# A hybrid encoder trunk on one core: the softmax shift folded into the low product of the scores, new orders in the attention, and the last down-projection turned round

## The reference

```
h = rms_norm(x); p = h @ W_in                       # 1024 -> 1952 columns
A: Hyena on 256 channels (FFT convolutions, gates)
B: GQA, 8 query heads, 2 key/value heads of 64      softmax(q k^T / 8) v
C: MLA, 4 heads, query/key 64 + 32 rotary, value 64 softmax(q k^T * 96^-0.5) v
x += rms_norm(concat(norm A, norm B, norm C) @ W_out)
h = rms_norm(x)
x += rms_norm((gelu(conv(h W_g)) * conv(h W_u)) @ W_down)   # 2816 wide inside
```

## Time and profile before

| | |
|---|---|
| median of 3 runs | 1431.39 us (1431.07 to 1433.14) |
| the profiled execution's own time | 1426.5 us |
| its span in the trace | 1424.7 us |
| PE busy | 1368.3 us, 96% of the span |
| DVE, ACT, POOL busy | 64%, 41%, 39% |

### The profile page before, as it was taken

The page is one execution under the profiler, slowest core; times in us unless marked ns, Lnnn a source line. Parts: engine busy times, 40 slices in busy tenths (PEclk is TensorE's granted clock), DMA queues, the critical chain, the costliest instruction groups (busy, mean ns, idle before and its releaser), DMA issues. The chain is left out here.

```text
span 1424.7 us, 15494 instructions
## 1 busy us (share of the span) xinstructions
PE 1368.3 (96%) x5988; PEld 1027.0 (72%) x5988; DVE 915.4 (64%) x992; ACT 587.7 (41%) x864; POOL 554.1 (39%) x287
## 2 busy tenths in 40 slices
PE   7999989999999999999989998998999999999998
PEld 5587654378888888788866785444888888887886
DVE  6776976547777787611286788665478877874213
ACT  5322455545543434422352225454464344343323
POOL 3221333046444444444552224320554444444444
PEclk9999999999999999999999999999999999999999
DMA  7313201022233333233341222110223333333332
GB/s 250 97 30 81 67 10 52 1 61 73 85 94 95 97 89 103 82 93 95 101 143 49 60 49 57 30 30 15 75 75 89 89 99 94 89 99 87 92 97 84
DMA packets 205538, 112.53 MB, mean 79 GB/s; under 512 B 15303, under 2 KB 202425, under 8 KB 204570
## 3 DMA queue, kind: packets, MB, share of 16 engines
q1 hardware_dynamic: 205466, 111.54, 27.0%
HBM read 105.63 MB, written 2.10 MB: 76 GB/s over the span
## 5 line engine op out<-in xcount | busy, mean ns | idle before, releaser
L527 POOL TENSOR_TENSOR wl<-raw,wh 128x1024 fp32r<-128x1024 f32 x172 | 421.5, 2451 | 628.2 <-ACT wh L611 628.2
L611 ACT ACTIVATE wh<-raw 128x1024 fp32r<-128x1024 f32 x172 | 182.1, 1059 | 519.8 <-PE ps L1140 493.8
L1138 PE MATMUL ps<-gh,wh 128*128 128x512 f32 (+1 forms) x848 | 340.7, 402 | 0.0
L1140 PE MATMUL ps<-gh,wl 128*128 128x512 f32 (+1 forms) x848 | 334.7, 395 | 0.0
L1139 PE MATMUL ps<-gl,wh 128*128 128x512 f32 (+1 forms) x848 | 334.6, 395 | 0.0
L1138 PEld LDWEIGHTS ps<-gh,wh 128*128 128x128 f32 (+1 forms) x848 | 158.3, 187 | 43.3 <-issue 3.9
L1139 PEld LDWEIGHTS ps<-gl,wh 128*128 128x128 f32 (+1 forms) x848 | 158.3, 187 | 40.5 <-issue 2.4
L1140 PEld LDWEIGHTS ps<-gh,wl 128*128 128x128 f32 (+1 forms) x848 | 158.2, 187 | 39.1
L1599 DVE TENSOR_TENSOR acc<-acc,sq 128x512 f32<-128x512 f32 x24 | 60.2, 2510 | 190.1 <-ACT sq L655 190.1
L2030 DVE SCALAR_TENSOR_TENSOR cv<-pad,pm,cv 128x512 f32<-128x512 f32 x88 | 127.4, 1447 | 70.0 <-ACT cv L989 70.0
L1138 PE MATMUL ps<-fh,wh 128*128 128x512 f32 x308 | 121.7, 395 | 0.6 <-POOL wl L527 0.6
(11 more groups left out here) (288 smaller groups left out, 2242.0 us busy)
## 6 DMA issues: line engine op xcount, KB each, us to landing
raw<-w_up SPq DMA_DIRECT2D x86, 512.0 KB, 3.8
raw<-w_down SPq DMA_DIRECT2D x32, 512.0 KB, 3.8
raw<-w_in SPq DMA_DIRECT2D x30, 512.0 KB, 4.1
raw<-w_out SPq DMA_DIRECT2D x16, 512.0 KB, 3.8
raw<-w_down SPq DMA_DIRECT2D x16, 384.0 KB, 3.4
xio<-x SPq DMA_DIRECT2D x4, 512.0 KB, 4.7
win<-c_win SPq DMA_DIRECT2D x2, 1024.0 KB, 5.5
TF<-c_tf SPq DMA_DIRECT2D x2, 1024.0 KB, 8.7
```

The costliest lines, as they stand in the source:

```text
L527: nc.gpsimd.tensor_tensor(l, raw[:, slot, :], h.bitcast(F32), ALU.subtract).then_inc(S["lo_ready"], 1)
L611: A(xh[:] if third(lay, n) else wh[:, slot, :], raw[:, slot, :], ACT.Copy).then_inc(S["hi_ready"], 1)
L1138: mm(ps[0:cols, bank, :], w_hi, x_hi, start=start and k == 0, stop=False)
L1140: ins = mm(ps[0:cols, bank, :], w_lo, x_hi, start=False, stop=stop and k == tile_n - 1)
```

## The change

**Scores.** `diag`, `shift` and the matmul of ones by `diag` are gone. The high half of a GQA head's keys still meets the packed query. The low half of the keys now meets a new tile `q3`: rows 0 to 63 hold the query (copied by POOL, `q_again`), rows 64 to 67 hold four rows, one for each block of 128 queries, with the negated maxima in that block and zero elsewhere; the keys' rows 64 to 67 are ones. So one matmul of 68 rows does the low product and the shift. An MLA head does the same in rows 96 to 99 of its one float32 matmul. To get the maxima as rows, PE multiplies the 128x4 tile `nm` by the identity (`turn_maxima`, 128 columns, float32, after `scores(h - 1, 3)`), and DVE spreads them (`max_row`).

**Orders.** `values(p, [2])` stays at the end of the even head; `values(p, [3])` moves to the odd head ahead of `denominators(p)`. In the last head `values(5, [0])` comes ahead of `denominators(4)`. Two of the four `mla_lo` subtractions move from DVE to POOL; the other two, `rotate_kr`, some `row_sums`, the squares and norms of the output groups and the splitting of the first two W_out items change places. `klo` writes each half once instead of twice, and ones into four rows.

**Layer 1's down-projection.** Its items are now 22 blocks of 128 rows of W_down. The activations are stationary and the weights move, so all 8 PSUM banks hold the result with tokens on partitions. The last two items are multiplied bank by bank, so that the banks end one after the other. ACT squares a bank with an accumulated sum, takes the logarithm and the exponential of one column, DVE applies gain and root and adds the old stream, and each of 8 pieces goes out. The old stream is transposed beforehand, four transposes at a time in eight of layer 1's feed-forward steps (`turn_stream`), and copied by ACT into buffers that are free.

The diff, cut to its core:

```
@@ pool
-                def shift(h):
-                    pool.wait_ge(S["nmax"], lay * N_TILES + (h + 1) * TC)
+                def q_again(h):
+                    pool.wait_ge(S["q2hi"], lay * GH + h + 1)
                     if h >= 2:
                         pool.wait_ge(S["s_tile"], lay * N_TILES + (h - 1) * TC)
-                    nc.gpsimd.tensor_tensor(diag[:, h % 2, :].rearrange("p (c n) -> p c n", c=TC), ..., ALU.mult)
+                    nc.gpsimd.tensor_copy(q3[0:GD, h % 2, :], qf[(h % 2) * GD:(h % 2 + 1) * GD, h // 2, :])
...
+                q_again(0)
+                q_again(1)
+                for k, (dst, src, hi_) in enumerate(((uql, uqr, uqh), (ukl, ukr, ukh))):
+                    nc.gpsimd.tensor_tensor(dst[:], src[:], hi_[:].bitcast(F32), ALU.subtract).then_inc(S["mlo_w"], 1)
                 q_lo(2)
@@ tensor
+                def turn_maxima(h):
+                    pe.wait_ge(S["nmax"], lay * N_TILES + (h + 1) * TC)
+                    mm(ps[ROW(h), N_BANK(h, TC - 1), 0:P], nm[:, h % 2, :], ident[:], start=True, stop=True)
...
                     if h < GH:
                         mm(ps[:, bank, :], ka[:, h // 4, keys], Q2[h % 3], start=True, stop=False)
-                        mm(ps[:, bank, :], kb[:, h // 4, keys], Q2[h % 3], start=False, stop=False)
+                    if sc == 0:
...
+                        pe.wait_ge(S["nm_row"], lay * HEADS + h + 1)
+                    if h < GH:
+                        ins = mm(ps[:, bank, :], kb[row, h // 4, keys], q3[row, h % 2, :], start=False, stop=True)
                     else:
-                        mm(ps[:, bank, :], mkf[0:MD, h - GH, keys], mqf[0:MD, h - GH, :], start=True, stop=False)
-                    if sc == 0:
-                        pe.wait_ge(S["shift"], lay * HEADS + h + 1)
-                    mm(ps[:, bank, :], ones_r[:], diag[:, h % 2, :], start=False, stop=True).then_inc(S["s_tile"], 1)
+                        ins = mm(ps[:, bank, :], mkf[row, h - GH, keys], mqf[row, h - GH, :], start=True, stop=True)
...
                     scores(h, 3)
+                    if after:
+                        turn_maxima(h + 1)
                     if whole:
-                        values(p, [2, 3])
+                        values(p, [2])
+                    if rest:
+                        values(p, [TC - 1])
+                    if h == HEADS - 1:
+                        values(PAIRS - 1, [0])
                     if rest:
                         denominators(p)
...
+                    if lay == DEPTH - 1 and 4 <= j < 20 and j % 2 == 0:
+                        turn_stream((j - 4) // 2)
...
+                for kk in range(FC - TAIL):
+                    ready(kk)
+                    for tt in (0, 2, 3, 1):
+                        for dh in range(2):
+                            ins = part(kk, tt, dh)
+                    ins.then_inc(S["pe_item"], 1)
+                for kk in range(FC - TAIL, FC):
+                    ready(kk)
+                for tt in range(TC):
+                    for dh in range(2):
+                        for kk in range(FC - TAIL, FC):
+                            ins = part(kk, tt, dh)
+                        ins.then_inc(S["y_done"], 1)
@@ vector
+                def max_row(h):
+                    dve.wait_ge(S["nm_tr"], lay * HEADS + h + 1)
+                    tt(dst.rearrange("p (c n) -> p c n", c=TC),
+                       ps[rows, N_BANK(h, TC - 1), 0:P].unsqueeze(1).to_broadcast([TC, TC, P]),
+                       ident[rows, rows].unsqueeze(2).to_broadcast([TC, TC, P]), ALU.mult).then_inc(S["nm_row"], 1)
@@ vector, after the layers
+            for i in range(TC):
+                for dh in range(2):
+                    dve.wait_ge(S["y_sq"], 2 * i + dh + 1)
+                    tt(ytmp[dh], ps[:, 2 * i + dh, :], cv[:, dh, :], ALU.mult).then_inc(S["y_gain"], 1)
+                dve.wait_ge(S["r_inv"], i + 1)
+                for dh in range(2):
+                    stt(out=x, in0=ytmp[dh], scalar=st[:, i, 4:5], in1=x, op0=ALU.mult, op1=ALU.add).then_inc(S["o_done"], 1)
```

More of the change, by code:

```diff
@@ L255, in build @@
             krs = sb("krs", [P, T], F32, s)
[L256 removed]
+            q3 = sb("q3", [P, 2, T], F32R, s)
             q2c = sb("q2c", [P, T], F32R, s)
@@ L264, in build @@
         ysave = probT0
+        xres = [rope[:, i, :] for i in range(5)] + [w3[:, 0:T], w3[:, T:2 * T], h2[:, 0:T]]
+        ytmp = [sq[:, 0, :], sq[:, 1, :]]
         groot = [rbc[:], cv[:, 1, :], rbc[:]]
@@ L502, in _ @@
             res = out.rearrange("b (c p) d -> p (b c) d", p=P)
[L503 to L507, removed]
+            for tt in range(TC):
+                for dh in range(2):
+                    sp.wait_ge(S["o_done"], 2 * tt + dh + 1)
+                    sp.dma_start(res[:, tt, dh * T:(dh + 1) * T], xres[2 * tt + dh]).then_inc(S["out_sem"], 16)
             sp.wait_ge(S["out_sem"], 16 * DC)
@@ L1009, in _ @@
                 tables("natural_log_exp_and_others")
+                if lay == DEPTH - 1:
+                    for n in range(I_DOWN + 3, LAST + 1):
+                        hi(lay, n, n % 2)
+                    continue
                 for m in range(DC):
@@ L1194, in gate @@
                             peaks(0, [k])
+                        if t == WIN - 1 and k == DC - 1:
+                            turn_maxima(0)
                     tiles(lay, t, t % 2, W_BANK[t], DC, gh, gl, 0, True, True, cols, gate)
@@ L1488, in _ @@
                         group(1)
-                values(PAIRS - 1, range(TC))
+                values(PAIRS - 1, range(1, TC))
                 denominators(PAIRS - 1)
@@ L1895, in _ @@
                 maxima(1)
+                max_row(1)
                 mla_lo(0)
-                mla_lo(2)
                 def group_sum(k):
@@ L1963, in _ @@
                         maxima(h + 1)
+                    if h == 3:
+                        row_sums(1)
+                    if h == 2 or h % 2 and h + 1 < HEADS and h != 7:
+                        max_row(h + 1)
                     if h in B7_FIRST and B7[B7_FIRST[h]][0] in ("pe", "v"):
@@ L1967, in _ @@
                         pair_out((h - 4) // 2)
-                    if h:
+                        if h + 1 < HEADS:
+                            max_row(h + 1)
+                    if h == 7:
+                        max_row(h + 1)
+                    if h == 3:
+                        mla_lo(1)
+                        rotate_kr()
+                    if h == 5:
+                        group_sum(0)
+                        group_sum(1)
+                    if h == 9:
+                        group_sum(2)
+                        group_sum(3)
+                    if h == 10:
+                        group_sum(5)
+                    if h == 11:
+                        group_norm(1, [0, 1])
+                    if h not in (0, 2, 11):
                         row_sums(h - 1)
```

242 lines of the change are left out of this document (141 added, 101 removed).

## The result

The kernel before took 1431.23 us (median of 4 runs, 1431.06 to 1433.14), the changed one 1399.37 us (4 runs, 1396.0 to 1401.27): ratio 0.9772, 95% interval [0.9748, 0.9796]. The forecast was 1410.1 us with a range of 1401 to 1422. On a second chip the same kernel had a ratio of 0.9816 [0.9788, 0.9845], 26 us. The profiled execution took 1401.19 us, its span 1399.3 us.

A forecast was written before the change was run, and what follows sets the result against it. PE, busy 96% of the span, was taken as the bound. Attention -18.2, feed-forward +4.2, last items +0.7 and end -8.0 summed to -21.3 us, from 1431.4 to 1410.1 us; range 1401 to 1422 us for 8 in 10.

The forecast's parts named there:

- clock term: Attention: three drops of the granted clock beside PE's holes go away, 1.7 us each, 5.1 us gained.
- (d): Attention: `max_row` on DVE delays the next head's second matmul, uncovered only in head 1, 0.7 us a layer.
- (f): Attention: other holes of PE grow, in head 1, in head 3 and before `group(1)`, 2.7 us a layer, +5.4 us.
- (a): Attention scores: 96 `diag` matmuls removed over both layers at 0.23 us each, -22.1 us.
- (b): Attention: 24 `turn_maxima` products on PE at 0.32 us each, +7.7 us.
- (c): Attention: PE's new wait before `turn_maxima`, 0.5 us in 16 GQA turns, 0.1 in 6 MLA turns; together +10 us.
- (e): Attention: holes of PE that close, 14.1 us, and clock drops that go with them, 5.1 us; sum -19.2 us.
- the holes hide one another: Rival, chance 0.13: PE's new stops let DVE and ACT catch up, (c) and (f) shrink by half, 1402 us.
- the clock falls through the 16 short stops: Rival, chance 0.08: short stops in GQA heads each bring the lower clock, 27 us added, 1437 us.
- DVE swallowing the gain: Rival, chance 0.15: each of 24 turns costs another half us, the attention gives 6.2 us, 1422 us.
- The tail: Layer 1's feed-forward transposes +4.2 us, wait for the last two down-projection items +0.7, shorter end -8.0.

The follow-up runs named there:

- no_turn: Changed kernel without turning the maxima and without spreading them, so the softmax is not shifted: 1386.0 us, ratio 0.9699 to the kernel before.
- orders_only: Kernel before with the new orders of DVE and ACT and the split values; scores, `diag` and low operands as they were: 1419.2 us, ratio 0.9935.
- attention_only: Kernel before with only the new attention (scores, orders, moved subtractions), old down-projection and end: 1403.4 us, ratio 0.9827.
- tail_only: Kernel before with only layer 1's new down-projection, the transposed stream and the new end, old attention: 1424.3 us, ratio 0.9977.
- lows_on_dve: Changed kernel with the low parts of two MLA weights subtracted by DVE again, not POOL: 1398.1 us, ratio 0.9787 to the kernel before.
- fill_hole: Changed kernel with one score product of head 3 made eight times instead of once, filling PE's stop there: 1396.2 us, ratio 0.9769 to the kernel before.

## Why the prediction was wrong

Compared at an equal clock, with the forecast's clock term apart and head 1's 1.4 us counted with (d), not with (f):

| term | forecast | measured | from |
|---|---|---|---|
| (a) products removed | -22.1 | -22.1, not measured alone | 96 x 0.23, by the starts in the trace |
| (b), (c), (d) the turn | +19.1 | +12.3 ± 1.4 | no_turn |
| (e) holes closed by orders (sums, `yl`, `cv`) | -6.8 | -8.8 ± 1.1 | orders_only |
| (e) `diag`, POOL's queries; (f) new holes | -3.3 | -7.8 | the rest of attention_only |
| (e) clock | -5.1 | +0.4 ± 2.4 | mean clock 0.9921 to 0.9916 |
| feed-forward, last items, end | -3.1 | -2.8 ± 0.8 | tail_only |

The attention without the clock was forecast at -13.1 us and measured at -26.4.

**The step that failed most is (c), with (b) and (d).** Nearly each number in it is in the trace: 0.49 us idle in a GQA head, next to none in an MLA head, 0.32 us to the next start; only the 0.4 us more in two odd heads a layer did not show, no stop there being longer than the others. What failed is the sum. I added 24 stops to a stream of PE that had other waits, as if none of them would shorten; 12.3 of the 19.1 us arrived. Of the 6.8 us that are missing, about 2 are these odd heads and a shorter wait for `max_row` (0.9 us for 1.4); the rest is stops that took the place of other waits. That was the forecast's own rival *the holes hide one another*, which halved (c) and (f) and gave 1402 us: by its mechanism the nearest of the cases, and still too small.

**(f) was too pessimistic, and the halved `klo` was put at nothing.** The wait at the first `bank7` item did not come: with POOL doing `uql` DVE is in time, as lows_on_dve shows by having that wait. The forecast noted the move and did not carry it into DVE's queue. In its place the stop of `peaks` in head 1 grew from 0.82 to 1.50 us in each layer, behind the `klo` that POOL holds up. The maxima of head 4 came 0.4 us later in layer 0 and 0.24 in layer 1, not 0.8. The forecast let `klo` cancel with other edits of DVE, "beside PE", though PE waited 1.5 us for it before; that wait is gone. By the lists of waits before and after this line of the table comes to -6.0 us: `diag` -4.4, POOL's queries -1.6 (forecast -2.9), `klo` -1.5 (forecast 0), `peaks` +1.5 (the forecast's (f) here +4.0). That leaves 1.8 us to the -7.8, which is a difference of three measured values with an uncertainty of about 2.3 us.

**The clock term had the right mechanism and the wrong sum.** The hole of 1.93 us and its drop are gone, as forecast; but (f) made a hole of 1.79 us in head 3, and I did not ask what the clock would do there. At the earlier trace rows a stop of 1.4 us between 200 and 210 us stood beside a clock of 1.00; the stop of 1.79 us there stands beside 0.83 or 0.66 in six profiles of six. This error of 5 us went against the other 13 us of the attention: that the time came out only 1.6 us below the range is in part luck. The rival that the clock falls through the 16 short stops is refuted: fill_hole has all 16 and a clock of 1.00 there. The Trainium skill ("TensorE: Matmul & The Clock Gate", A second HAM failure mode) describes a clock that swings with frequent small idle times; here stops of 0.3 to 0.9 us left it alone in these slices, and one of 1.79 us did not.

**DVE swallowing the gain** did not happen: no stop before a turn is over 0.33 us in the list. **The tail** was right in all its terms: 5.4 us for 5.6 at the end, +3.6 for +4.2 in the feed-forward, 0.7 for 0.7.

**The first measurement's extra.** 27.8 us at an equal clock plus the clock's +0.4 make 27.4, against 31.9 measured first. Its kernel before ran at 1431.2 us, where 37 later runs have a median of 1428.4. The clocks of those four runs are not listed, so that this is the clock's doing is only argued.

## What to carry to other kernels

A new stop on an engine that already waits elsewhere costs less than its length: take it out by an experiment before its full sum goes into a forecast, or carry it through the next wait on the list. When a change moves operations from one engine's queue to another's, go through the queue again for each wait that you forecast behind it. Where TensorE is the bound and has one long stop, compare the granted clock of that slice in several profiles; splitting the stop, or filling it with harmless products, took the drop away here and was worth about 2 us. Look at more than one profile, since drops come and go between executions of the same kernel. And before an operation is put down as lying beside the bounding engine, look for it in the list of waits: `klo` was there with 1.5 us.

## What the hardware showed that was not expected

- Time against clock: over 104 runs 0.87 us for each 0.001 of the mean granted clock, with 1.3 us of scatter left. Comparing at an equal clock told about 1.5 to 2 us apart with 4 or 5 runs.
- One stop of 1.79 us went with a drop in 6 of 6 profiles, the same idle time in two pieces of 0.90 and 0.84 us never; 1.61 us of useless products in the stop took the drop away in both layers, worth about 2 us of 1400 by the profiles (219.4 to 217.3 us) and by the mean clock of all kernels with and without the stop (1.8 ± 1.4 us). Stops of 1.5 us went with a drop in 7 of 20 cases.
- A second float32 product of 4 by 128 columns starts 0.22 us behind the first; from a single one to the next work of another form it is 0.32 us. Twenty-four of them more, 5.3 us by the starts, lengthened the attention by 3.8 us in the profile.
- `klo`'s two operations on DVE took 2.79 us beside two subtractions on POOL and 1.39 us without them.
- ACT's square with an accumulated sum is followed by a read of the accumulator of 0.19 us.
